# Seven block products for the input matmuls of a first FFN, with twenty modulation units at its output slabs

## The reference

```
mod = silu(c) @ w_ada[l] + b_ada[l]            # 6 x 1024 values a layer, for latents and for context
h   = rmsnorm(x, norm_ffn[l]) * (1 + sc2) + sh2
g,u = split(h @ w_in[l])                       # w_in: 1024 x 5632, so g and u: 768 x 2816
x   = x + g2 * ((silu(g) * u) @ w_out[l])      # w_out: 2816 x 1024
```

## Time and profile before

| | |
|---|---|
| runs of the kernel, median (lowest to highest) | 1621.3 us (1621.28 to 1621.32) |
| span of the profiled execution, first to last instruction | 1618.6 us |
| between the span and the median run | 2.7 us |
| PE busy / DVE busy / ACT busy | 1582.3 / 920.9 / 575.2 us |
| mean granted clock of TensorE | 0.992 of full speed |
| first FFN from the start of slab F0 + 3 to the start of KV0 | 484.0 to 998.4 us |

### The profile page before, as it was taken

One profiled execution on the slowest core, in us unless ns is written; L12 is line 12 of the kernel. 1 busy time (PEld: TensorE's weight loads), 2 busy tenths in 40 slices (PEclk: granted clock), 3 DMA queues, 4 the chain that ended last, 5 costly groups with the idle time before them and its releaser, 6 DMA issues.

```text
span 1618.6 us, 23967 instructions
## 1 busy us (share of the span) xinstructions
PE 1582.3 (98%) x9424; PEld 1345.5 (83%) x9424; DVE 920.9 (57%) x1592; ACT 575.2 (36%) x829; POOL 100.3 (6%) x95
## 2 busy tenths in 40 slices
PE   7999999999999999999999999989999999999998
PEld 5789988888888888888888888877778888888886
DVE  5665536544576667556666555888856533333334
ACT  5225457542342111122102124567744431222222
POOL 0000000000000000000000000046630000000003
PEclk8999999999999999999999999999999999999999
DMA  9442300013234334433343413320002323332332
GB/s 334 117 132 71 113 27 27 27 53 105 79 105 129 119 122 123 128 119 116 130 125 109 130 59 111 109 74 1 2 27 79 104 85 97 104 99 83 104 91 91
DMA packets 197438, 156.20 MB, mean 97 GB/s; under 512 B 6754, under 2 KB 194318, under 8 KB 197358
## 3 DMA queue, kind: packets, MB, share of 16 engines
q1 hardware_dynamic: 197358, 155.10, 31.5%
HBM read 149.84 MB, written 2.10 MB: 94 GB/s over the span
## 4 chain that ended last, share of the span: by engine, by line
PE 86%; DVE 5%; ACT 5%; issue 1%; DMA 1%; SPq 1%; DVEq 0%; ACTq 0%
PE ps L609 84%; PE ps L1145 1%; ACT pr L1703 1%; DVE w_lo L1749 1%; DMA ada_pre<-in_w_ada 1%; DVE scaled L1803 1%; DVE h_lo L1812 1%; ACT w_hi L1260 1%; PE ps L1150 1%; SPq L407 0%; DVE row_max L2394 0%; DVE q_st L2339 0%; ACT h_hi L1310 0%; DMA w_raw<-in_ffn_w_out 0%; ACT r_act L1460 0%
## 5 line engine op out<-in xcount | busy, mean ns | idle before, releaser
L609 PE MATMUL ps<-h_hi,w_hi 128*128 128x512 f32 (+1 forms) x1392 | 499.9, 359 | 1.4 <-DVE w_lo L1749 1.4
L609 PE MATMUL ps<-h_lo,w_hi 128*128 128x512 f32 (+1 forms) x1392 | 490.6, 352 | 0.0
L609 PE MATMUL ps<-h_hi,w_lo 128*128 128x512 f32 (+1 forms) x1392 | 490.4, 352 | 0.0
L1749 DVE TENSOR_TENSOR w_lo<-w_raw,w_hi 128x2048 fp32r<-128x2048 f32 (+1 forms) x88 | 197.1, 2240 | 201.9 <-ACT w_hi L1260 201.9
L609 PEld LDWEIGHTS ps<-h_hi,w_hi 128*128 128x128 f32 x1392 | 263.7, 189 | 47.0 <-issue 10.7
L1260 ACT ACTIVATE w_hi<-w_raw 128x2048 fp32r<-128x2048 f32 (+1 forms) x88 | 165.2, 1877 | 374.4 <-DMA w_raw<-in_ffn_w_in 200.0
L609 PEld LDWEIGHTS ps<-h_hi,w_lo 128*128 128x128 f32 x1392 | 263.6, 189 | 36.3
L609 PEld LDWEIGHTS ps<-h_lo,w_hi 128*128 128x128 f32 x1392 | 264.0, 190 | 35.7
L609 PE MATMUL ps<-a_hi,w_hi 128*128 128x512 f32 (+1 forms) x528 | 187.9, 356 | 0.1
L609 PE MATMUL ps<-a_lo,w_hi 128*128 128x512 f32 (+1 forms) x528 | 186.9, 354 | 0.0
L609 PE MATMUL ps<-a_hi,w_lo 128*128 128x512 f32 (+1 forms) x528 | 186.7, 354 | 0.0
(11 more groups left out here) (264 smaller groups left out, 1986.8 us busy)
## 6 DMA issues: line engine op xcount, KB each, us to landing
w_raw<-in_ffn_w_in SPq DMA_DIRECT2D x88, 512.0 KB, 4.9
ada_w<-in_w_ada SPq DMA_DIRECT2D x41, 1024.0 KB, 5.2
w_raw<-in_ffn_w_out SPq DMA_DIRECT2D x32, 512.0 KB, 4.4
w_raw<-in_gla_w_in SPq DMA_DIRECT2D x24, 512.0 KB, 4.9
ada_pre<-in_w_ada SPq DMA_DIRECT2D x7, 1024.0 KB, 11.6
w_raw<-in_ffn_w_out SPq DMA_DIRECT2D x16, 384.0 KB, 3.6
w_raw<-in_gla_w_o SPq DMA_DIRECT2D x8, 512.0 KB, 6.8
w_raw<-in_swa_w_o SPq DMA_DIRECT2D x8, 512.0 KB, 4.7
```

What stands on the lines that cost most here:

```text
L609: return pe.matmul(o, w, r, start=start, stop=stop, skip_group_check=skip)
L1749: dve.tensor_tensor(w_lo[s][:, 0:kc, :], raw_of(n)[:, 0:kc, :], w_hi[s][:, 0:kc, :].bitcast(F32), ALU.subtract).then_inc(wlo_ok, 1)
```

## The change

**Input slabs.** The first three input slabs of the first FFN stay as they were. In the other 19, the 1024 features and the two column blocks (gate, up) are seen as 2 x 2 blocks, the 768 tokens as two halves of 384, and the product of 2 x 2 by 2 x 2 blocks is computed with seven block products in place of eight. A product is 4 steps x 3 parts = 12 matmuls of 384 columns (`product`). For this three weights of the seven are blocks as loaded, and four are sums of blocks that VectorE makes (`form_sum`); each of the seven is split into high and low (`form_high` on ScalarE, `form_low` on VectorE, 128 x 512 each). The tokens' sums are made once: ScalarE also writes h unsplit (`h_full`), VectorE makes four sums of quarters (128 x 1536), and they are split too. Products that belong to several results are copied or added from PSUM after the fact (`part_sum` on ScalarE; `gate_sum_one`, `gate_sum_two`, `up_sum_one`, `up_sum_two` on VectorE, 128 x 384 each) before silu and multiply.

**Parts.** `a_hi` and `a_lo` shrink to four steps, so the 22 input slabs stand in six parts (`PARTS0`: 4, 4, 4, 3, 3, 4), each with 4 output slabs: 24 output slabs of 3 or 4 steps in place of 12 of 6 or 8. The output matmuls are as many as before.

**Units.** The 28 units stand at the last input slab of each of the first five parts, at all 4 output slabs of these parts (20), and at three input slabs of the last part. `unit_sum` moves to the following slab, and `store_sum` with it, in front of the next `unit_acc`.

The core of the diff:

```diff
-KV0 = F0 + FFN_SLABS
+PARTS0 = [(0, 4), (4, 4), (8, 4), (12, 3), (15, 3), (18, 4)]
+HT = T // 2
+SEVEN, IN0, OUT0, UNIT_AT = {}, {}, {}, {}
+for part_, (f_, fc_) in enumerate(PARTS0):
+    n_ = F0 + f_ + 4 * part_
+    for j_ in range(fc_):
+        IN0[n_ + j_] = f_ + j_
+        if f_ + j_ >= 3:
+            SEVEN[n_ + j_] = f_ + j_ - 3
+        if part_ == 0 and j_ == 3 or 0 < part_ < 5 and j_ == fc_ - 1 or part_ == 5 and j_ > 0:
+            UNIT_AT[n_ + j_] = 12 + len(UNIT_AT)
+    for e_ in range(4):
+        OUT0[n_ + fc_ + e_] = (part_, e_, fc_)
+        if part_ < 5:
+            UNIT_AT[n_ + fc_ + e_] = 12 + len(UNIT_AT)
+assert len(UNIT_AT) == 28
+KV0 = F0 + FC + 4 * len(PARTS0)
...
+    def form_from(n, j, raw, sums):
+
+        q = SEVEN[n]
+        return (block_of(raw, n % 2, 0, 0), sums[0][:, :, :], block_of(raw, n % 2, 1, 0), sums[1][:, :, :],
+                block_of(raw, n % 2, 1, 1), sums[2][:, :, :], sums[3 + q % 2][:, :, :])[j]
+
...
-        ffn(0, F0)
+        for n in range(F0, KV0):
+            if n in IN0:
+                load_slab(n, 0, gate_up(ffn_w_in[0], IN0[n]))
+            else:
+                part, e, fc = OUT0[n]
+                load_slab(n, 0, cols(ffn_w_out[0], e * 256, fc, PARTS0[part][0] * P))
+            if n in UNIT_AT:
+                load_unit(UNIT_AT[n])
...
+        def product(n, j):
+
+            q, s = SEVEN[n], n % 2
+            if j == 0:
+                pe.wait_ge(out_free[s], n // 2)
+            if q == 0 and j in (1, 3, 4, 5):
+
+                pe.wait_ge(sl_ok, (1, 3, 4, 5).index(j) + 1)
+            if j in (3, 4, 5):
+
+                pe.wait_ge(sn_ok, 4 * q + j - 2)
+            if j == 6:
+                pe.wait_ge(g_ok, q + 1)
+            pe.wait_ge(fl_ok, 7 * q + j + 1)
+            o = bank(slab_banks(n) + (0, 1, 2, 0, 1, 0, 2)[j], 0, HT)
+            low = form_from(n, j, w_lo, t_lo)
+            x_hi, x_lo = token_form(j)
+            for k in range(4):
+                for i, (w, x) in enumerate(((form_hi[j], x_hi), (form_hi[j], x_lo), (low, x_hi))):
+                    last = mm(o, w[:, k, :], x[:, k, :], start=(k == 0 and i == 0 and j in (0, 1, 2, 6)),
+                              stop=(k == 3 and i == 2), skip=True)
+            last.then_inc(pd_ok if j < 6 else slab_done, 1)
...
+        for n in range(F0 + 3, KV0):
+            if n in SEVEN:
+                for j in range(7):
+                    product(n, j)
+                    if j == 1 and n - 1 in UNIT_AT:
+                        unit_sum(UNIT_AT[n - 1])
+            else:
+                part, e, fc = OUT0[n]
+                done = PARTS0[part][0] + fc
+
+                def ready(k, done=done, fc=fc):
+
+                    if k in (0, fc - 1):
+                        pe.wait_ge(a_ok, done - (k == 0))
+                slab(n, 0, a4_in, BOTH, kc=fc, k_wait=ready,
+                     before={(0, 1): lambda: unit_sum(UNIT_AT[n - 1])} if n - 1 in UNIT_AT else {})
 
...
                     act.activation(h_hi[:, ch, s[0]:s[1]], scaled_t[ch % 2][:, s[0]:s[1]], ACT.Identity,
                                    bias=mods[:, sh + ch, int(s == CTX):int(s == CTX) + 1]).then_inc(hh_ok, 1)
+                if l == 1:
+                    for s in segs:
+                        last = act.activation(h_full[:, ch, s[0]:s[1]], scaled_t[ch % 2][:, s[0]:s[1]], ACT.Identity,
+                                              bias=mods[:, sh + ch, int(s == CTX):int(s == CTX) + 1])
+                    last.then_inc(hf_ok, 1)
```

ScalarE's and VectorE's parts:

```diff
+        def form_high(n, j):
+
+            q, s = SEVEN[n], n % 2
+            if n - 1 in SEVEN:
+                act.wait_ge(pd_ok, 6 * (q - 1) + j + 1) if j < 6 else act.wait_ge(slab_done, n)
+            elif j > 2:
+                act.wait_ge(slab_done, n)
+            if j in (0, 2, 4):
+                act.wait_ge(in_w[s], 32 * (n // 2 + 1))
+            else:
+                act.wait_ge(ts_ok, 4 * q + {1: 1, 3: 2, 6: 3, 5: 4}[j])
+            act.activation(form_hi[j][:, :, :], form_from(n, j, w_raw, t_sum), ACT.Copy).then_inc(fh_ok, 1)
...
+        def part_sum(n, i):
+
+            q, s, b0 = SEVEN[n], n % 2, slab_banks(n)
+            act.wait_ge(pd_ok, 6 * q + (1, 2, 4, 6)[i])
+            if i == 1:
+
+                act.wait_ge(a_ok, IN0[n] - 1)
+            dst = (tmp[s][:, 0:HT], tmp[2 + s][:, HT:T], tmp[2 + s][:, 0:HT], tmp[s][:, HT:T])[i]
...
+        def form_sum(n, i):
+
+            q, s = SEVEN[n], n % 2
+            if i == 0:
+                dve.wait_ge(in_w[s], 32 * (n // 2 + 1))
+            if n - 1 in SEVEN and i != 2:
+
+                dve.wait_ge(pd_ok, 6 * (q - 1) + (2, 4, 0, 6)[i])
+            elif i == 2 and q >= 2:
+
+                dve.wait_ge(slab_done, n - 1 if n - 1 in SEVEN else n - 4)
+            if i in (1, 2):
+                dve.wait_ge(ts_ok, 4 * q + i)
+            a, b = ((block_of(w_raw, s, 0, 1), block_of(w_raw, s, 0, 0)), (block_of(w_raw, s, 1, 1), t_sum[0][:, :, :]),
+                    (block_of(w_raw, s, 1, 0), t_sum[1][:, :, :]),
+                    (block_of(w_raw, s, 1, 1), block_of(w_raw, s, 0, 1)))[i]
+            dve.tensor_tensor(t_sum[(0, 1, 3 + q % 2, 2)[i]][:, :, :], a, b, ALU.subtract).then_inc(ts_ok, 1)
+
+        def form_low(n, j):
+
+            dve.wait_ge(fh_ok, 7 * SEVEN[n] + j + 1)
+            dve.tensor_tensor(form_from(n, j, w_lo, t_lo), form_from(n, j, w_raw, t_sum), form_hi[j][:, :, :].bitcast(F32),
+                              ALU.subtract).then_inc(fl_ok, 1)
...
+        for n in range(F0 + 3, KV0):
+            a_ = UNIT_AT.get(n)
+            last_a = UNIT_AT.get(n - 1)
+            if n in SEVEN:
+                after = n + 1 in SEVEN
...
+                    form_low(n, 5)
+                    form_low(n, 6)
+                if after:
+                    form_sum(n + 1, 0)
+                    form_low(n + 1, 0)
+                gate_sum_one(n)
+                if last_a is not None:
+                    store_sum(last_a)
+                if after:
+                    form_sum(n + 1, 1)
+                    form_sum(n + 1, 2)
+                    form_low(n + 1, 1)
+                    form_low(n + 1, 2)
+                    up_sum_one(n)
+                    if a_ is not None:
+                        unit_acc(a_)
+                    form_low(n + 1, 3)
+                    form_sum(n + 1, 3)
+                    up_sum_two(n)
+                    form_low(n + 1, 4)
+                    form_low(n + 1, 5)
+                else:
+                    if a_ is not None:
+                        unit_acc(a_)
+                    up_sum_one(n)
+                    split(n + 1, 0, OUT0[n + 1][2])
+                    up_sum_two(n)
+                gate_sum_two(n)
+                if after:
+                    form_low(n + 1, 6)
+                times_gate(n)
+                low0(n)
+            else:
+                part, e, fc = OUT0[n]
+                if last_a is not None:
+                    store_sum(last_a)
+                if part == 5 and e == 0:
+                    scale_rows(48 + 8, V_NMIX + 8)
+                if a_ is not None:
+                    unit_acc(a_)
+                if e < 3:
+                    split(n + 1, 0, fc)
+                elif part < 5:
+                    form_sum(n + 1, 0)
+                    form_low(n + 1, 0)
+                    form_sum(n + 1, 1)
+                    form_sum(n + 1, 2)
+                    form_low(n + 1, 1)
+                else:
+                    split(n + 1)
+                if part < 5:
+                    residual(n, 0, BOTH, 40, 2 * e, None)
+                    if e == 3:
+                        form_low(n + 1, 2)
+                else:
+                    plain(n, "ffn0", 2 * e, 40, BOTH, False)
+                    for ch in range(2):
```

More of the change, by code:

```diff
@@ L1069, in ffn @@
                     for e in range(2):
[L1070 removed]
+                        slab(n + e, i, a_in, segs, kc=fc, k_wait=ready)
                 if l == 1 and after:
@@ new lines, in _ @@
+        last.then_inc(out_free[0], 1)
+        normal(1, 0, BOTH, sh, 6, 8)
+        split(n + 2)
+        dve.wait_ge(out_free[0], n // 2 + 1)
+        dve.wait_ge(sg_ok, 1)
+        for sg in BOTH:
+            c_ = int(sg == CTX)
+            last = dve.scalar_tensor_tensor(tmp[2][:, sg[0]:sg[1]], tmp[2][:, sg[0]:sg[1]], bz[:, 1, c_:c_ + 1],
+                                            tmp[0][:, sg[0]:sg[1]], ALU.add, ALU.mult)
+        last.then_inc(zp_ok, 1)
+        low0(n)
+        dve.wait_ge(hf_ok, DC)
```

298 lines of the change are left out of this document (253 added, 45 removed).

## The result

| | before | changed |
|---|---|---|
| runs, median (lowest to highest) | 1621.29 us (1621.04 to 1621.32) | 1679.69 us (1676.98 to 1682.38) |
| ratio to before, 95% interval | | 1.036 (1.0344 to 1.0375) |
| span of the profiled execution | 1618.6 us | 1679.4 us |
| start of KV0, the end of the first FFN | 998.37 us | 1059.36 us |

A forecast was written before the change was run, and what follows sets the result against it. TensorE bounds the kernel before; in the changed output slabs, one buffer's transfer plus unit_acc would. Terms -39 + 75 + 11 + 5 + 1 + 3 + 7 = +63 on 1621.3 us gave 1685 us, 8-in-10 range 1652 to 1718.

The forecast's parts named there:

- TensorE, -39: 19 input slabs of seven products: 84 matmuls at 174 ns, 14.6 us a slab, 2.1 us less each, saving 39 us.
- Output slabs with units, +75: Five parts' output slabs: transfer and unit_acc in a row on one buffer, 11.6 us per unit; 236 us for TensorE's 161.
- The last part's three input slabs, +11: Three successive input slabs with units: VectorE needs 19 us with waits, 4 us too much each, less a slab's lead.
- Slab F0 + 3, +5: At slab F0 + 3 VectorE's sums, splits, first forms and unit take 36.3 us where TensorE needs 31.3.
- Heads, +1: At five heads of parts (first input slabs), VectorE's additions stand before the third form: +1 us.
- the clock, +7: Some 25 TensorE pauses of 2.5 to 4.7 us lower its clock: +7 us, with ends 0 and 42 us.
- the end of 42 us: Upper end of the clock term: 25 pauses at up to 1.7 us each.
- The rival of 1710: Clock falls at each pause on the path, or small VectorE instructions cost 5% more: +15 to +35 us; chance 0.20.
- The start, +3: Before 466.67 us, ScalarE writes h a second time, 0.42 us over its idle time in each of eight steps: +3 us.
- The rival that TensorE stays the bound (1585): Units take under 8.9 us each, output slabs run at TensorE's pace, the 39 us come through: 1585 us; chance 0.04.
- The rival of 1658: Only VectorE's own work counts: 10.6 us an output slab for 11.6 (-20), no clock term (-7); about 1658 us; chance 0.16.

The follow-up runs named there:

- The fill experiment: Changed kernel with 12 or 24 dummy matmuls of 384 columns on TensorE after each of the 20 output slabs that carry a unit; 1675.3 us.

## Why the prediction was right

Step by step, with the profile's sections from the start of F0 + 2 to KV0:

- **TensorE, -39: right.** Matmuls of 384 columns follow each other at 173 ns (below: 18 of them in 3.12 us); 174 were taken as the middle of 120 and 227. The Trainium skill's formula for an isolated matmul (TensorE: Matmul & The Clock Gate, section Back-to-back issue gap) gives 162 by estimate, and the trace of this stream is above it at this size too. Shown again in the kernel without units: 14.6 us a slab. TensorE's timeline of the changed kernel, every third matmul of an input slab:

```profile
671.10 0.33 PE L677 MATMUL ps<-h_hi,form_hi 128*128 128x384 f32 x1
...
674.22 0.33 PE L677 MATMUL ps<-h_hi,form_hi 128*128 128x384 f32 x1
```

- **Output slabs with units, +75: right, with two limits where I had one.** 47.0 us a part were measured for 47.2, in sum 234.9 for 236. The transfer and `unit_acc` in a row are one limit (half a transfer: -18.7 us, half of `unit_acc`: -70.2 us, both in the range expected from this sum). The other, VectorE waiting for sums that TensorE makes late at its lower clock, I had only in the clock term; it gives nearly the same cycle (11.4 to 11.7 us where it shows by itself, with half a transfer).
- **The last part's three input slabs, +11: 13.5, by another way.** The four slabs took 73.5 us where matmuls and sums alone make 60.0. I had VectorE's work as a sum and full speed on TensorE. What the trace has is 7.1 us of pauses, which go over ScalarE, whose copies stand behind a form, and 6.4 us by which TensorE's work took longer, at a granted clock of 0.92. An order of SyncE's that the chain put forward was no cause.
- **Slab F0 + 3, +5: right.** 503.86 - 467.85 = 36.0 us against 31.3.
- **Heads, +1, and the clock, +7: 5 together for the input sections** (211.6 us for 206.6 of matmuls and sums). The fill experiment puts the clock at 4.4 us in the output slabs and behind them, which excludes the end of 42 us; what it cost in the last part lies in the term above and is open, so the clock's term may have been too small. The rival of 1710 is excluded by the measured time itself.
- **The start, +3: about +1.** F0 + 2 began at 467.85 in place of 466.67. In the kernel before without units, whose start is not changed at all, it began at 468.7, so this term is within what the start varies by.
- **Missed: +1.6 before KV0.** With four steps in place of six, the last output slabs are shorter than the load and split of KV0's weights. It shows in every kernel here (2.6 us without units); I had said that transfers keep their work and not asked what the shorter slabs in front of one no longer cover.

In sum -39 + 75 + 11 + 5 + 1 + 7 = +60 was predicted for this stretch, and 591.5 - 531.7 = +59.8 measured; with the start 63 (the prediction rounded 1684.3 up to 1685) and 61. That the sum agrees to a microsecond is partly luck: the last part and KV0 were 4 us short, and the other terms as much too long. The signs that were to show it came: slabs of 3 and of 4 steps take the same time, VectorE waits for the transfer up to 1.6 us, TensorE's busy time falls from 531.7 to 528.6 us while the stretch gets longer, and input slabs in the middle of a part do not wait for their forms (40.0 of 40.0 us busy from 560 to 600 us). The first input slab of a part did wait for its forms, 0.9 to 3.4 us, behind the unit of the output slab before it; that wait is part of the 11.5 us. One sign against it came twice in fifteen: a transfer that had landed before VectorE was ready, by 0.07 and 0.39 us. The rival that TensorE stays the bound (1585) is the kernel without units (1584.4), but not for the reason I gave: I let the whole 39 us come through and kept the 15 us of sums, while without units the sums are gone and 14 us go to waits at the seams. The rival of 1658 took 1 us off each of 20 output slabs; by the prediction's own terms only the 15 that follow another have the 11.6 us, which makes it 1663.

## What to carry to other kernels

When a change makes the bound engine's pieces shorter, list everything that ran beside one piece with a fixed length (a transfer and its reader on one buffer, a load with its split, a tail at a seam) and compare each with the new length. Here 11.6 us against 8.9 and 6.8 cost 74 us at the output slabs, and the shorter input slabs had gained 39. Where two limits lie within a few tenths of each other, removing one shows little (the clock, 4.4 us), and removing the other leaves the first in some places (with half a transfer, four units of fifteen still came after 11.4 us or more), so test each alone, and both together. And work that moves from a busy engine to the bound one can still pay, if it is priced by start to start: 1.7 us on TensorE bought 7 us on VectorE and 5 us of the buffer.
